# Gated attention: query blocks 0 and 1 joined to one unit on TensorE, compressed steps and value products placed anew, more room for exponentials

## The reference

```
q = partial_rope(q.reshape(b, s, C_HEADS, HEAD_DIM), cos, sin)
s_c = einsum('bqghd,bngd->bghqn', qb, kc) * scale       # 31 compressed keys
p_c = masked_softmax(s_c, cmp_end[None, :] <= t[:, None])
o_c = einsum('bghqn,bngd->bqghd', p_c, vc)
s_s = einsum('bqghd,bgqkd->bghqk', qb, k_g) * scale     # selected keys
p_s = masked_softmax(s_s, valid_s[:, :, None])
o_s = einsum('bghqk,bgqkd->bqghd', p_s, v_g)
s_w = einsum('bqghd,bkgd->bghqk', qb, kw) * scale       # window keys
p_w = masked_softmax(s_w, valid_w)
o_w = einsum('bghqk,bkgd->bqghd', p_w, vw)
out = gb[..., 0:1] * o_c + gb[..., 1:2] * o_s + gb[..., 2:3] * o_w
```

## Time and profile before

| | us |
|---|---|
| median of 3 runs | 2269.31 (2268.11 to 2269.79) |
| the profiled execution | 2269.1 |
| its span | 2267.8 |
| TensorE busy in the span | 2211.9 (98%) |
| VectorE busy | 1344.5 (59%) |
| ScalarE busy | 560.3 (25%) |

### The profile page before, as it was taken

How to read it: one execution, slowest core, us unless ns; L and a number is a source line. 1 busy time by engine, 2 the same in 40 slices (tenths; PEclk the granted TensorE clock), 3 DMA queues, 4 the chain that set the end, 5 groups by cost and what they waited for, 6 DMA issues and landing times.

```text
span 2267.8 us, 29576 instructions
## 1 busy us (share of the span) xinstructions
PE 2211.9 (98%) x10990; PEld 1585.1 (70%) x10990; DVE 1344.5 (59%) x3432; ACT 560.3 (25%) x1421; POOL 199.3 (9%) x210
## 2 busy tenths in 40 slices
PE   9999999999999999999999999999999999999997
PEld 7776578888888885558888888888867643333333
DVE  6777756656566667886665666767776522222224
ACT  2223431101001206772110000333572111111111
POOL 0013430000000002330000000000020011111011
PEclk9999999999999999999999999999999999999999
DMA  5211032232223320002222222232205899999997
GB/s 212 75 57 47 13 124 85 83 93 89 79 93 92 116 75 20 1 1 75 76 93 93 78 90 93 76 103 65 65 11 223 347 421 423 423 423 424 424 424 310
DMA packets 60207, 346.54 MB, mean 153 GB/s; under 512 B 9248, under 2 KB 10144, under 8 KB 42208
## 3 DMA queue, kind: packets, MB, share of 16 engines
q1 hardware_dynamic: 55360, 335.03, 39.6%
q0 software_dynamic: 3840, 6.46, 0.8%
q10 hardware_dynamic: 864, 3.15, 0.3%
HBM read 337.59 MB, written 17.30 MB: 156 GB/s over the span
## 4 chain that ended last, share of the span: by engine, by line
PE 86%; DMA 9%; DVE 2%; ACT 1%; issue 1%; SPq 0%; DVEq 0%; POOLq 0%; ACTq 0%
PE bank L634 30%; DMA places<-in_experts 8%; PE bank L640 8%; PE bank L647 8%; PE bank L655 8%; PE bank L3051 6%; PE bank L3059 3%; PE bank L623 2%; PE bank L1100 2%; PE bank L1085 2%; PE bank L1112 2%; PE bank L3008 1%; PE bank L729 1%; PE bank L3024 1%; PE bank L497 1%; PE bank L1307 1%
## 5 line engine op out<-in xcount | busy, mean ns | idle before, releaser
L3051 PE MATMUL bank<-places,xT 128*64 128x512 f32 x824 | 184.0, 594 | 13.9 <-DMA places<-in_experts 13.9
L3260 DVE TENSOR_SCALAR square<-bank,mt 128x256 f32<-128x256 f32 x32 | 15.5, 484 | 288.0 <-ACT rope L3163 288.0
L3051 PEld LDWEIGHTS bank<-places,xT 128*64 128x64 f32 x824 | 59.3, 137 | 133.0 <-issue 117.9
L1961 DVE TENSOR_TENSOR third<-first,bank 128x256 f32<-128x256 f32 x106 | 44.7, 421 | 150.9 <-PE bank L634 150.2
L634 PE MATMUL bank<-u,ring 128*128 128x256 f32 x540 | 130.3, 381 | 1.1 <-DVE y_ab L1995 1.1
L634 PE MATMUL bank<-h,ring 128*128 128x256 f32 x512 | 120.9, 379 | 0.0
L634 PE MATMUL bank<-h_sums,w_sum 128*128 128x256 f32 x512 | 120.9, 379 | 0.0
L2652 POOL TENSOR_SCALAR exps<-exps,small,gates 128x128 f32<-128x128 f32 (+1 forms) x64 | 56.4, 882 | 657.6 <-DVE small L2446 657.6
L634 PEld LDWEIGHTS bank<-u,ring 128*128 128x128 f32 x540 | 101.2, 190 | 17.8 <-issue 3.3
L634 PE MATMUL bank<-u_mlp_sums,w_sum 128*128 128x256 f32 x480 | 113.4, 379 | 0.0
L634 PE MATMUL bank<-u_mlp,ring 128*128 128x256 f32 x480 | 113.4, 379 | 0.0
(11 more groups left out here) (556 smaller groups left out, 4406.2 us busy)
## 6 DMA issues: line engine op xcount, KB each, us to landing
places<-in_experts SPq DMA_DIRECT2D x56, 2048.0 KB, 35.1
ring<-in_dense SPq DMA_DIRECT2D x216, 512.0 KB, 4.2
places<-in_experts SPq DMA_DIRECT2D x40, 1024.0 KB, 26.2
x<-in_experts SPq DMA_DIRECT2D x12, 1024.0 KB, 37.8
w<-in_experts SPq DMA_DIRECT2D x10, 1024.0 KB, 32.1
consts<-in_experts SPq DMA_DIRECT2D x10, 1024.0 KB, 32.9
x<-in_experts SPq DMA_DIRECT2D x4, 2048.0 KB, 33.5
consts<-in_consts SPq DMA_DIRECT2D x1, 2310.5 KB, 16.4
```

What stands on the lines that cost most here:

```text
L3051: ins = k.pe.matmul(bank[a * CAP:(a + 1) * CAP, :], xT[:, kk % 4, kk // 4, :], w[:, (2 * (kk % 2) + a) * EH:(2 * (kk % 2) + a + 1) * EH], ...
```

## The change

The blocks 0 and 1 of a branch form one unit; blocks 2 and 3 are units of their own (`NSA_UNITS`, three a branch, six a pair). On TensorE a step is now a unit: both blocks' logits one behind the other, into the same two banks at columns 0 and 128, and their transposes together, head 0 of both and then head 1 of both. Transposes stand three units behind the logits. The compressed transposes and the rotation product are both at unit 3 of a pair, the compressed values at unit 4, and the value products of a branch stand behind the transposes of the next branch's joined unit. ScalarE follows the same units, with its copy of the compressed weights at unit 3. VectorE and GpSimd keep their order. The exponentials' buffer grows from 6 x 512 to 10 x 512 columns, room for eight blocks.

```diff
@@ -366,7 +366,8 @@
         k.hs = [sb(f"h{q}", [P, KT, T], stack=st) for q in range(2)]
         k.us["h"] = [quarters(sb(f"h_sums{q}", [P, 6, T], stack=st), 3) for q in range(2)]
     with ExitStack() as st:
-        exp_buffers(k, st)
+        exp_buffers(k, st, 10)
+        k.ec = k.eb.rearrange("p b t -> p (b t)")
         k.us["c"] = quarters(k.eb, 3)
         k.yc = sb("y_c", [P, N_C, T], stack=st)
         ce = sb("weights_c", [P, 16, T], stack=st)
@@ -414,8 +415,8 @@
     return [ap[:, 2 * i:2 * i + 2, :].rearrange("p a (h t) -> p (a h) t", t=HT) for i in range(n)]
 
 
-def exp_buffers(k, st):
-    k.eb = k.sb("exps", [P, 6, T], stack=st)
+def exp_buffers(k, st, n=6):
+    k.eb = k.sb("exps", [P, n, T], stack=st)
     k.E = [k.eb[:, b, :] for b in range(6)]
 
 
@@ -457,6 +458,7 @@
 TURN_LAG = 3
 SOFT = FOX + DSA
 NSA = [(m, x, b) for m in range(8) for x in range(2) for b in range(NB)]
+NSA_UNITS = [tuple(NB * g + b for b in blocks) for g in range(16) for blocks in ((0, 1), (2,), (3,))]
 DA = [(h, b) for h in range(4) for b in range(NB)]
 
 
@@ -1052,53 +1054,76 @@
 
     pe, s = k.pe, k.s
     pe.wait_ge(s["combined"], 2 * (CH_C // 2 + N_C // 2 - 1))
-    for step in range(len(NSA) + 5):
-        if step < len(NSA):
+    for step in range(len(NSA_UNITS) + 4):
+        if step < len(NSA_UNITS):
             pe_nsa_logits(k, step)
         if step == 0:
             pe.wait_ge(s["scaled"], SCALED["c"] + N_C)
-        m, at = divmod(step, 8)
+        m, at = divmod(step, 6)
         if m < 8 and at == 0:
             pe_cmp_logits(k, m)
-        if 0 <= step - 3 < len(NSA):
+        if 0 <= step - 3 < len(NSA_UNITS):
             pe_nsa_turn(k, step - 3)
-        if m < 8 and at == 4:
+        if m < 8 and at == 3:
             pe_cmp_turn(k, m)
-        if m < 7 and at == 5:
+        if m < 7 and at == 3:
             pe.wait_ge(s["scaled"], SCALED["c"] + CQ + m + 2)
             pe_rope(k, k.ch7, ("cq", m + 1), k.yc[:, CQ + m + 1, :])
-        if m < 8 and at == 6:
+        if m < 8 and at == 4:
             pe_cmp_values(k, m)
-        if 0 <= step - 4 < len(NSA) and NSA[step - 4][2] == NB - 1:
-            pe_nsa_values(k, step - 4)
-
-
-def pe_nsa_logits(k, n):
+        if step >= 4 and (step - 4) % 3 == 2:
+            pe_nsa_values(k, NSA_UNITS[step - 4][-1])
+
+
+def nsa_unit(n):
+
+    return 3 * (n // NB) + max(0, n % NB - 1)
+
+
+def nsa_at(n):
+
+    return P if n % NB == 1 else 0
+
+
+def nsa_turns(n, a):
+
+    unit = NSA_UNITS[nsa_unit(n)]
+    return 2 * unit[0] + a * len(unit) + unit.index(n) + 1
+
+
+def nsa_logits(k, n, a):
+
+    return k.bank[2 * (nsa_unit(n) % 2) + a][:, nsa_at(n):]
+
+
+def pe_nsa_logits(k, u):
     pe, s = k.pe, k.s
-    m, x, b = NSA[n]
-    if n >= 2:
-        pe.wait_ge(s["c_masked"], 2 * (n - 1))
-    if n % 8 == 0:
-        pe.wait_ge(s["roped"], ROPED["cq", m])
+    if u >= 2:
+        pe.wait_ge(s["c_masked"], 2 * (NSA_UNITS[u - 2][-1] + 1))
+    for n in NSA_UNITS[u]:
+        m, x, b = NSA[n]
+        if n % 8 == 0:
+            pe.wait_ge(s["roped"], ROPED["cq", m])
+        for a in range(2):
+            r = slice(a * HD, (a + 1) * HD)
+            pe.matmul(nsa_logits(k, n, a)[:, 0:P * (b + 1)], k.yc[r, CQ + m, b * P:(b + 1) * P], k.yc[r, (KS, KW)[x], 0:P * (b + 1)],
+                      start=True, stop=True).then_inc(s["c_lg_done"], 1)
+
+
+def pe_nsa_turn(k, u):
+    pe, s = k.pe, k.s
     for a in range(2):
-        r = slice(a * HD, (a + 1) * HD)
-        pe.matmul(logits_bank(k, n, a)[:, 0:P * (b + 1)], k.yc[r, CQ + m, b * P:(b + 1) * P], k.yc[r, (KS, KW)[x], 0:P * (b + 1)],
-                  start=True, stop=True).then_inc(s["c_lg_done"], 1)
-
-
-def pe_nsa_turn(k, n):
-    pe, s = k.pe, k.s
-    m, x, b = NSA[n]
-    for a in range(2):
-        if n:
-            pe.wait_ge(s[f"c_turned{a}"], n)
-        if (n, a) == (1, 0):
-            pe_keep(k, k.bank[4], 8)
-        pe.wait_ge(s[("c_scaled", "c_scaled_1")[a]], n + 1)
-        e = sized_tile(k, n, b, a)
-        for j in range(b + 1):
-            ins = pe.transpose(k.bank[4 + a][:, j * P:(j + 1) * P], e[:, j * P:(j + 1) * P], k.const("ident"))
-        ins.then_inc(s["c_t_done"], 1)
+        for n in NSA_UNITS[u]:
+            m, x, b = NSA[n]
+            if u and n == NSA_UNITS[u][0]:
+                pe.wait_ge(s[f"c_turned{a}"], n)
+            if (n, a) == (1, 0):
+                pe_keep(k, k.bank[4], 8)
+            pe.wait_ge(s[("c_scaled", "c_scaled_1")[a]], n + 1)
+            e, at = nsa_tile(k, n, b, a), nsa_at(n)
+            for j in range(b + 1):
+                ins = pe.transpose(k.bank[4 + a][:, at + j * P:at + (j + 1) * P], e[:, j * P:(j + 1) * P], k.const("ident"))
+            ins.then_inc(s["c_t_done"], 1)
 
 
 def pe_nsa_values(k, n):
@@ -1603,6 +1628,12 @@
     return k.eb.rearrange("p b t -> p (b t)")[:, at:at + P * (b + 1)]
 
 
+def nsa_tile(k, n, b, a):
+
+    at = P * (20 * (n // NB % 2) + 10 * a + b * (b + 1) // 2)
+    return k.ec[:, at:at + P * (b + 1)]
+
+
 def soft_columns(k, n):
 
     q = 2 * (n % 8)
@@ -1677,21 +1708,21 @@
 
 def act_nsa(k):
     act, s = k.act, k.s
-    for step in range(len(NSA) + 5):
-        m, at = divmod(step, 8)
-        n = step - 3
-        if 0 <= n < len(NSA):
-            act_nsa_turned(k, n)
-        if step < len(NSA):
-            act_exps(k, step, NSA[step][2], "c_masked", "c_exp_done", sized_tile)
-        if m < 8 and at == 0:
-            act.wait_ge(s["cmp_shifted"], m + 1)
-            act.activation(k.pc, k.pc, ACT.Exp).then_inc(s["cmp_exp"], 1)
-        if m < 8 and at == 4:
+    for step in range(len(NSA_UNITS) + 4):
+        m, at = divmod(step, 6)
+        if 0 <= step - 3 < len(NSA_UNITS):
+            for n in NSA_UNITS[step - 3]:
+                act_nsa_turned(k, n)
+        if step < len(NSA_UNITS):
+            for n in NSA_UNITS[step]:
+                act_exps(k, n, NSA[n][2], "c_masked", "c_exp_done", nsa_tile)
+                if n % 8 == 0:
+                    act.wait_ge(s["cmp_shifted"], m + 1)
+                    act.activation(k.pc, k.pc, ACT.Exp).then_inc(s["cmp_exp"], 1)
+        if m < 8 and at == 3:
             act_take(k, k.ch7, ("cmpT", m), k.pcT.rearrange("p h q -> p (h q)"), k.ch7.bank[:, 0:2 * P])
-        n = step - 4
-        if 0 <= n < len(NSA) and n % 8 == 7:
-            act_take(k, k.ch6, ("nsa", n // 8), k.u[:, n // 8, :], k.ch6.bank)
+        if step >= 4 and (step - 4) % 6 == 5:
+            act_take(k, k.ch6, ("nsa", (step - 4) // 6), k.u[:, (step - 4) // 6, :], k.ch6.bank)
 
 
 def nsa_weights_free(k, eng, n):
@@ -1708,9 +1739,9 @@
     m, x, b = NSA[n]
     nsa_weights_free(k, act, n)
     for a in range(2):
-        act.wait_ge(s["c_t_done"], 2 * n + a + 1)
+        act.wait_ge(s["c_t_done"], nsa_turns(NSA_UNITS[nsa_unit(n)][-1], a))
         act.copy(k.ceT[x][a][:, 0:b + 1, b * P:(b + 1) * P],
-                 k.bank[4 + a][:, 0:P * (b + 1)].rearrange("p (j t) -> p j t", t=P)).then_inc(s[f"c_turned{a}"], 1)
+                 k.bank[4 + a][:, nsa_at(n):nsa_at(n) + P * (b + 1)].rearrange("p (j t) -> p j t", t=P)).then_inc(s[f"c_turned{a}"], 1)
 
 
 def act_2_among(k, i):
@@ -2416,8 +2447,10 @@
     for step in range(len(NSA) + 5):
         m, at = divmod(step, 8)
         if step < len(NSA):
-            free = (s["c_t_done"], 2 * (step - 4) + 1, 1) if step >= 4 else None
-            dve_masks(k, step, NSA[step][2], causal(k, NSA[step][2]), "c_lg_done", "c_masked", free, SCALE, sized_tile)
+            unit = NSA_UNITS[nsa_unit(step)]
+            free = (s["c_t_done"], nsa_turns(step - 8, 0), len(unit)) if step >= 8 else None
+            dve.wait_ge(s["c_lg_done"], 2 * (unit[-1] + 1))
+            dve_masks(k, step, NSA[step][2], causal(k, NSA[step][2]), "c_lg_done", "c_masked", free, SCALE, nsa_tile, nsa_logits)
         if m < 8 and at == 0:
             dve_cmp_logits(k, m)
         if 0 <= step - 2 < len(NSA):
@@ -2445,7 +2478,7 @@
     dve.wait_ge(s["c_exp_done"], 2 * n + 2)
     k.inverted.append(own.link(dve.reciprocal(inv, total)))
     dve.wait_ge(own.sem, k.inverted[n])
-    e, q = sized_tile(k, n, b, 0), 6 * m + 1 + x
+    e, q = nsa_tile(k, n, b, 0), 6 * m + 1 + x
     dve.tensor_scalar(e, e, inv[:, 0:1], k.gt[:, b, q:q + 1], ALU.mult, ALU.mult).then_inc(s["c_scaled"], 1)
 
 
@@ -2647,7 +2680,7 @@
     pool, s = k.pool, k.s
     for n, (m, x, b) in enumerate(NSA):
         neg, total, inv = soft_columns(k, n)
-        e, q = sized_tile(k, n, b, 1), 6 * m + 4 + x
+        e, q = nsa_tile(k, n, b, 1), 6 * m + 4 + x
         pool.wait_ge(k.dve_own.sem, k.inverted[n])
         pool.tensor_scalar(e, e, inv[:, 1:2], k.gt[:, b, q:q + 1], ALU.mult, ALU.mult).then_inc(s["c_scaled_1"], 1)
 
```

## The result

The changed kernel takes 2296.59 us (median of 4 runs, 2292.24 to 2302.37), the kernel before 2268.71 (median of 4 runs, one more than in the table further up); the ratio is 1.0121, interval 1.0106 to 1.0137. The profiled execution has a span of 2299.1 us, 31.3 more than before.

The account below looks back on a forecast made before the run. TensorE, busy 159.66 of 172 us, sets the attention stage's end. Waits of 14.9 (six periods) + 0.4 (first pair) + 2 (last) = +17 us and clock +9 us, on 2269.1, gave 2295, range 2279 to 2309.

Parts of the forecast that it names:

- The late copy: Rotation on TensorE waits for ScalarE's copy of the compressed weights, 2.9 us in each of seven pairs.
- The first wait: Joined transposes of blocks 0 and 1 wait for VectorE's scaling of block 1, 1.3 us a pair.
- The chain from block 2's logits to the rotation: From block 2's logits at 5.22 us into the pair to the rotation near 15.3.
- The buffers: Twice the room for exponentials is worth 0, since masks wait only for TensorE's logits.
- the joined logits: Two blocks' logits on TensorE, counted as 1.05 us a unit.
- often V: Said a half pair's value products often stood between compressed transposes and rotation in the kernel before.
- The clock: TensorE's clock falls in seven stretches before the rotation, 1.3 us each, +9 us; ends 0 and 24 us.
- The first pair: No value products ahead of block 2's logits or behind the rotation: +0.4 on its 18.73 us.
- The end: Last pair has no rotation, keeps the first wait, later value products: between 0 and +3, taken as +2 us.
- Rival 2: The two waits with the clock held at 1.00: 2286, 2280 to 2291; chance 0.35.
- rivals 3 and 4: 3: only the first wait, copy not late, 2268, chance 0.04. 4: neither wait, 2257, chance 0.04.
- Rival 5: The clock falls and stays low over two such stretches' work: 2308 to 2320; chance 0.05.

Follow-up runs that it names:

- experiment 1: Changed kernel with the rotation product one unit later, at unit 4 of a pair: 2267.11 us, 0.9994 of the kernel before.
- experiment 5: Changed kernel with a branch's value products one step later, behind the logits of block 2 or block 6: 2290.37 us, 1.0087.
- experiment 4: Kernel before with only the exponentials' buffer enlarged and the masks' release wait eight blocks back: 2267.56 us, 0.9997.
- experiment 3: Changed kernel with nine extra unused products on TensorE between compressed transposes and rotation: 2279.25 us, 1.0042.
- experiment 8: Changed kernel with copy ahead of exponentials, value products one step later, rotation behind block 6's logits: 2260.49 us, 0.9961; run again 2260.56 us, 0.9961.
- experiment 7: Changed kernel with the compressed weights' copy ahead of the exponentials and the rotation behind the same step's value products: 2262.98 us, 0.9971.
- experiment 2: Changed kernel with ScalarE's copy of the compressed weights ahead of the exponentials of blocks 4 and 5: 2275.89 us, 1.0029.
- experiment 6: Kernel before with only the rotation product moved right behind the compressed transposes, nothing joined: 2289.78 us, 1.0086.

## Why the prediction was right

- The late copy: forecast seven waits of 2.9 us, measured seven of 2.8, and with the rotation moved (experiment 1) the loss is gone. Shown.
- The first wait: forecast 1.3 us, measured up to 1.37 once a pair. Experiment 5 shows that the place of the value products ahead of block 2's logits makes about half of it.
- The chain from block 2's logits to the rotation: forecast 10.1 us, measured 10.0.
- The buffers: forecast 0, measured a ratio of 0.9997 (experiment 4).
- A size that was off: I gave the joined logits the sum of two blocks, 1.05, and the joined transposes 0.81; at the pair's start they take 0.85 and 0.67. So block 2's logits start 4.86 us into the pair (904.85 to 909.71) and not 5.22. In the pair's middle the shorter logits give nothing, because the transposes behind them wait for VectorE's chain, which starts at block 2's logits. With 0.1 us less up to the rotation a period costs 2.01 us more than before (experiment 3), not 2.48.
- A reading that was wrong: that "often V" stood between the compressed transposes and the rotation in the kernel before. In its rows (907.52 to 909.00) only block 5's logits and block 2's transposes do. The sum doesn't use it.
- The clock fell in all seven stretches, as forecast, but I priced a fall at 1.3 us; the six periods show 2.26 each. Three periods are 24.53 or 24.54 us, 1.65 over experiment 3's 22.89; the others are 25.31, 25.97 and 26.00, and in them the low clock lasts about twice as long: the windows of 5 us show 0.66 once (970 to 975), but 0.87, 0.50 and 0.94 in a row from 940 to 955. The sum allowed for such a doubling at its upper end, not in its middle.
- The first pair: forecast +0.4 and one of the seven falls at 1.3, so +1.7; measured +1.43. Experiment 3 splits it otherwise: its first pair takes 18.63 us, 0.1 less than before, so the fall is 1.53 and the new order costs nothing there. The end: +2 forecast, +1.85 measured.
- Outside the stage I forecast nothing, and 2.4 us are there: 3.7 ahead of it, -1.3 behind. In the profiled execution the granted clock is also below 1.00 at 210, 810 and 1830 us, before it was so at 290 us only. Such falls differ between executions of one kernel: experiment 8 was run twice with the same kernel, and the clock at 810 us was 1.00 in one trace and 0.66 in the other, whose stage starts 4.8 us later (860.14 against 855.30). The fall at 1830 us does not account for the -1.3, which stay open.

Over six periods my waits came out 2.8 us too high and the clock 5.8 us too low. In the stage I had 26.3 us and the trace shows 28.9. The total (2295) came within 2 us of the median (2296.59), but that is in part luck: two errors of opposite sign, and a median 3.8 us under the profiled execution (2300.41). Rival 2 is refuted by the clock rows, rivals 3 and 4 by the waits. Rival 5 had the low clock last over two stretches' work; it did so in three of the six periods only, and the total stayed under its 2308.

## What to carry to other kernels

When steps are fused on the engine that sets the end, walk every product that shares a bank through the other engine's new order: what empties the bank may now stand behind twice the work. Price an idle stretch on TensorE by its wait and by the clock after it; here the new order cost 2.01 us a period and the clock 2.26. Where a wait can't be avoided, unused products in it can hold the clock (experiment 3). In this stage a product that needs a copy did best behind the long products that don't (experiments 7 and 8).

## What the hardware showed unasked

- Four logits products with 64 rows each, issued back to back, take 0.85 us; as two pairs with other work between they took 0.42 + 0.63. Joining is a gain of its own, of 0.2 us a unit. For transposes no such gain is shown: six in one group take 0.67 us behind the compressed logits and 0.81 for block 2 in the same kernel, and no run separates the causes.
- A fall of the granted clock costs the same in two orders of the stage. The period with the shorter low stretch is 1.65 us longer (24.54 against 22.89, and 22.81 against 21.16 in experiment 2), the one with a low stretch of twice that length 3.0 to 3.1 (25.97 and 24.17). One period of the changed kernel (25.31) lies between.
- Short waits can be followed by a fall: one came at waits for the copy of 1.5 us in three of seven pairs (experiment 6), and of 1.1 us in two of seven (experiment 2). The wait for the scaling was 1.4 us in both experiment 2 and experiment 7, and the clock never fell in the stage of experiment 7. What decides between the cases is not shown.
- The spread of the runs does not tell whether the clock falls in the stage. The changed kernel spread over 10 us with seven falls (2292.24 to 2302.37), but experiment 5, also with seven, over 3 us, and the kernel before, with none in its trace, over 10 us when it ran 26 times (2265.3 to 2274.94).
